# State-space tiles of a two-block layer: decay blocks in three buffers, the subtract of the next tile while on this one

## What is computed

```python
def step(state, inp):                       # one chunk of M_CHUNK = 128 tokens; 8 of them
    xc, ac, bc, cc = inp
    acum = jnp.cumsum(ac, axis=1)
    seg = jnp.where(causal, acum[:, :, None] - acum[:, None, :], -jnp.inf)
    scores = jnp.einsum('btgn,bsgn->btsg', cc, bc)[..., None] * jnp.exp(seg)
    y_diag = jnp.einsum('btsgh,bsghp->btghp', scores, xc)
    y_off = jnp.einsum('btgn,bghpn->btghp', cc, state) * jnp.exp(acum)[..., None]
    w_end = jnp.exp(acum[:, -1:] - acum)
    new_state = (state * jnp.exp(acum[:, -1])[..., None, None]
                 + jnp.einsum('bsgn,bsghp->bghpn', bc, xc * w_end[..., None]))
    return new_state, y_diag + y_off
```

## Time and profile before

| what | value |
|---|---|
| device time, median of 3 runs | 3124.95 us (3123.76 to 3127.22) |
| device time of the profiled execution | 3125.96 us |
| its span | 3124.3 us |
| PE busy | 2945.9 us (94%) |
| DVE busy | 1750.8 us (56%) |
| ACT busy | 1009.9 us (32%) |
| POOL busy | 414.3 us (13%) |
| mean granted PE clock | 0.972 |

### The profile page before, as it was taken

The page is one execution under the profiler, slowest core; times in us unless marked ns, Lnnn a source line. Parts: engine busy times, 40 slices in busy tenths (PEclk is TensorE's granted clock), DMA queues, the critical chain, the costliest instruction groups (busy, mean ns, idle before and its releaser), DMA issues.

```text
span 3124.3 us, 39886 instructions
## 1 busy us (share of the span) xinstructions
PE 2945.9 (94%) x16263; PEld 2297.6 (74%) x16263; DVE 1750.8 (56%) x1912; ACT 1009.9 (32%) x1309; POOL 414.3 (13%) x461
## 2 busy tenths in 40 slices
PE   2998999999999999999898999999979998999989
PEld 2885656667788888888777887878767886666667
DVE  5566726662455455543585747567454227676773
ACT  2123435551211111111233424234333114444452
POOL 0002000001011111100101112021101001332340
PEclk7998999999999999999899999999979999999999
DMA  6355011011133333321124223242311221212021
GB/s 229 108 169 132 4 28 29 8 28 41 48 115 120 115 101 111 116 76 47 36 65 128 80 83 107 68 135 75 107 56 37 98 88 61 68 35 68 35 74 61
DMA packets 245528, 249.16 MB, mean 80 GB/s; under 512 B 14021, under 2 KB 208418, under 8 KB 245378
## 3 DMA queue, kind: packets, MB, share of 16 engines
q1 hardware_dynamic: 221664, 170.39, 18.0%
q0 software_dynamic: 17680, 58.89, 6.3%
q10 hardware_dynamic: 6034, 17.74, 1.5%
HBM read 218.17 MB, written 26.45 MB: 78 GB/s over the span
## 4 chain that ended last, share of the span: by engine, by line
PE 79%; DVE 11%; issue 4%; ACT 4%; DMA 1%; ACTq 0%; SPq 0%; DVEq 0%
PE PU L973 16%; PE PU L975 16%; PE PU L974 16%; PE PM L1614 2%; PE PU L1592 2%; PE PU L1284 2%; DVE small L2757 2%; PE PM L1602 2%; PE PM L1634 2%; PE PM L1636 2%; PE PM L1635 2%; PE PU L987 2%; PE PU L1216 1%; PE PU L988 1%; PE PU L989 1%
## 5 line engine op out<-in xcount | busy, mean ns | idle before, releaser
L973 PE MATMUL PU<-hH,w_hi_t 128*128 128x512 f32 (+1 forms) x1872 | 739.1, 395 | 2.4 <-DVE w_lo_t L2349 2.4
L975 PE MATMUL PU<-hH,w_lo_t 128*128 128x512 f32 (+1 forms) x1872 | 730.7, 390 | 0.0
L974 PE MATMUL PU<-hL,w_hi_t 128*128 128x512 f32 (+1 forms) x1872 | 729.9, 390 | 0.0
L2349 DVE TENSOR_TENSOR w_lo_t<-w_raw,w_hi_t 128x1024 fp32r<-128x1024 f32 x181 | 228.6, 1263 | 357.4 <-ACT w_hi_t L1746 345.3
L973 PEld LDWEIGHTS PU<-hH,w_hi_t 128*128 128x128 f32 (+1 forms) x1872 | 351.4, 188 | 77.0 <-DVE w_lo_t L2349 3.8
L975 PEld LDWEIGHTS PU<-hH,w_lo_t 128*128 128x128 f32 (+1 forms) x1872 | 350.8, 187 | 76.0
L974 PEld LDWEIGHTS PU<-hL,w_hi_t 128*128 128x128 f32 (+1 forms) x1872 | 351.4, 188 | 72.2
L1746 ACT ACTIVATE w_hi_t<-w_raw 128x1024 fp32r<-128x1024 f32 x167 | 174.5, 1045 | 458.0 <-PE PU L975 356.3
L2825 DVE SCALAR_TENSOR_TENSOR xT<-PU,mod,xT 128x1024 f32<-128x1024 f32 x120 | 154.0, 1283 | 202.5 <-PE PU L975 202.5
L3106 DVE TENSOR_TENSOR_SCAN s_keep<-s_keep,zero 128x128 f32<-128x128 f32 (+7 forms) x128 | 180.6, 1411 | 2.0 <-POOL s_keep L928 2.0
L928 POOL TENSOR_SCALAR_AFFINE_SELECT s_keep<-s_keep 128x128 f32<-128x128 f32 x128 | 114.5, 910 | 501.5 <-ACT s_keep L2237 500.9
(11 more groups left out here) (419 smaller groups left out, 5003.8 us busy)
## 6 DMA issues: line engine op xcount, KB each, us to landing
ada_w<-in_ada_w_dram POOLq DMA_DIRECT2D x64, 384.0 KB, 4.0
w_raw<-in_w_gu_dram SPq DMA_DIRECT2D x44, 512.0 KB, 3.8
w_raw<-in_m_in_w_dram SPq DMA_DIRECT2D x40, 512.0 KB, 3.9
ada_w<-in_w_ada_dram POOLq DMA_DIRECT2D x32, 512.0 KB, 4.6
seg<-decay_sums SPq DMA_DIRECT2D x32, 512.0 KB, 4.7
w_raw<-in_w_down_dram SPq DMA_DIRECT2D x22, 512.0 KB, 3.4
w_raw<-in_w_in_dram SPq DMA_DIRECT2D x17, 512.0 KB, 3.9
ada_w<-in_w_ada_dram SPq DMA_DIRECT2D x16, 512.0 KB, 18.8
```

The lines of the kernel that those rows point to most:

```text
L973: mm(PU[0:width, up, half, :], whi, aH[:, k, cols], start=k == 0, stop=False)
L974: mm(PU[0:width, up, half, :], whi, aL[:, k, cols], start=False, stop=False)
L975: last = mm(PU[0:width, up, half, :], wlo, aH[:, k, cols], start=False, stop=k == kt - 1)
L2349: V.tensor_tensor(w_lo_t[:, p, 0:w], w_raw[:, p, 0:w], w_hi_t[:, p, 0:w].bitcast(F32), ALU.subtract)\
```

## The change

The blocks `seg` get a third buffer, tile c uses buffer c % 3. On SP the DMA of tile j+1's block is issued in step j, behind the factors and the panel of step j, for j = 1 to 6 (tiles 0 and 1 as before). On VectorE the subtract of tile c+1 stands in step c, behind `output(c-2)` and the split and ahead of `masked(c)`; that of tile 0 stands ahead of the loop. The masking of the scores into `cbm` moves from `segments` into `masked`, directly ahead of the multiply. On ScalarE the high part of a panel and the copy of a z unit are each issued ahead of the next tile's Relu and Exp. PE's order is the same.

```diff
-        seg = at("seg", A + 11264, [P, 2, 8, P])
+        seg = [at(f"seg{n}", o, [P, 8, P]) for n, o in enumerate((A + 11264, A + 12288, A + 16384))]
@@ SP
             def tile_decays(i, j):
+                if j >= 2:
+                    sp.wait_ge(bc_landed[j % 2], 16 * (4 * i + j // 2))
+                if j >= 3:
+                    sp.wait_ge(ss_y, TT * i + j - 2)
...
-                sp.dma_start(seg[:, j % 2, :, :].rearrange("p h t -> p (h t)"), src).then_inc(bc_landed[j % 2], 16)
+                sp.dma_start(seg[j % 3][:, :, :].rearrange("p h t -> p (h t)"), src).then_inc(bc_landed[j % 2], 16)
@@
                 for j in range(TT):
-                    if j >= 2:
-                        sp.wait_ge(ss_y, TT * i + j - 1)
-                    tile_decays(i, j)
-                    if j >= 2:
+                    if j < 2:
+                        tile_decays(i, j)
+                    else:
                         sp.wait_ge(ss_g, TT * i + j - 1)
                     tile_factors(i, j)
...
+                    if 1 <= j < TT - 1:
+                        tile_decays(i, j + 1)
@@ ScalarE
+                if i == 0:
+                    activate(i, 5)
+                decays(i, 0)
                 for c in range(TT):
-                    if c == 0 and i == 0:
-                        activate(i, 5)
-                    decays(i, c)
                     if c % 2 == 0:
                         split()
                     else:
                         p = unit()
                         free(af(zf[:, c // 2, :], unit_ps(p), ACT.Silu if last else ACT.Copy))
+                    if c + 1 < TT:
+                        decays(i, c + 1)
@@ VectorE
             def segments(i, c):
...
                                 acum[:, c, 8 * i:8 * i + 8].unsqueeze(2).broadcast_to([P, 8, P]), ALU.subtract).then_inc(ss_seg, 1)
+
+            def masked(i, c):
                 ve.wait_ge(ss_cb, TT * i + c + 1)
                 if TT * i + c:
                     ve.wait_ge(ss_m, TT * i + c)
                 V.tensor_tensor(cbm[:, :], PM[:, 3, 0:P], tri[:, :], ALU.mult).then_inc(ss_cbr, 1)
-
-            def masked(i, c):
                 ve.wait_ge(ss_exp, TT * i + c + 1)
@@
+                segments(i, 0)
                 for c in range(TT):
                     if c >= 2:
                         state_update(i, c - 2)
                         output(i, c - 2)
-                    segments(i, c)
                     if c % 2 == 0:
                         split()
                         skip()
+                    if c + 1 < TT:
+                        segments(i, c + 1)
                     masked(i, c)
```

More of the change, by code:

```diff
@@ L1482, in ssd_out @@
                         last = mm(PM[hd * HD:(hd + 1) * HD, 0, f * P:(f + 1) * P], xdt[:, h * HD:(h + 1) * HD],
-                                  seg[:, c % 2, h, :], start=True, stop=True)
+                                  seg[c % 3][:, h, :], start=True, stop=True)
                 last.then_inc(ss_y, 1)
@@ L2143, in decays @@
                 act.wait_ge(ss_seg, TT * i + c + 1)
-                s2 = seg[:, c % 2, :, :].rearrange("p h t -> p (h t)")
+                s2 = seg[c % 3][:, :, :].rearrange("p h t -> p (h t)")
                 link(af(s2, s2, ACT.Relu, scale=-1.0))
@@ L2932, in segments @@
                 ve.wait_ge(bc_landed[b], 16 * (4 * i + c // 2 + 1))
-                V.tensor_tensor(seg[:, b, :, :], seg[:, b, :, :],
+                V.tensor_tensor(seg[c % 3][:, :, :], seg[c % 3][:, :, :],
                                 acum[:, c, 8 * i:8 * i + 8].unsqueeze(2).broadcast_to([P, 8, P]), ALU.subtract).then_inc(ss_seg, 1)
+            def masked(i, c):
                 ve.wait_ge(ss_cb, TT * i + c + 1)
@@ L2938, in segments @@
                 V.tensor_tensor(cbm[:, :], PM[:, 3, 0:P], tri[:, :], ALU.mult).then_inc(ss_cbr, 1)
-            def masked(i, c):
                 ve.wait_ge(ss_exp, TT * i + c + 1)
                 ve.wait_ge(ss_cbr, TT * i + c + 1)
-                V.tensor_tensor(seg[:, c % 2, :, :], seg[:, c % 2, :, :], cbm[:, :].unsqueeze(1).broadcast_to([P, 8, P]),
+                V.tensor_tensor(seg[c % 3][:, :, :], seg[c % 3][:, :, :], cbm[:, :].unsqueeze(1).broadcast_to([P, 8, P]),
                                 ALU.mult).then_inc(ss_m, 1)
```

## The result

The changed kernel takes 3224.99 us (median of 4 runs, 3221.67 to 3226.57), the kernel before 3124.36 in the same comparison: a ratio of 1.0323, with a 95% interval of 1.0305 to 1.0341. It is 3.2% slower, some 101 us; 3228 was predicted. The span of its profiled execution is 3220.0 us, 95.7 more than that of before.

The account below looks back on a forecast made before the run. PE was taken as the bound. Scans before output(5) add 94 us and the ends 9, together 103 on the profiled 3126: 3229, less 1 for the median, 3228; range 3190 to 3268.

Parts of the forecast that it names:

- The bound: PE, busy 94% of the span, bounds the kernel; at 8.67 us a tile, some 27 us is the most won.
- The loop: Scans, c = 2 to 6: output(c-2), SP's issues, block landing, VectorE to output(c-1); 12.9 us a tile, 14.6 with a panel.
- the panel's term: Block behind factors and a panel on SP: issued at 2.51 us instead of 1.96, landing 6.1 us instead of 4.9.
- VectorE's part: VectorE behind the block's landing: subtract 1.13, mask 0.3, multiply to the end of output(c-1) 4.59 us.
- the upper end of the range: 3268 us: VectorE's instruction lengthened once a loop (+17), a panel's landing 6.8 (+6), half the way to (c).
- The skill's fit: Block's DMA by 2.0 us and 436 GB/s: 3.2 us for 512 KB instead of 4.9, the sum 34 us lower.
- PE in the loop: PE is in time with 5 us to spare and idles 4.2 us a tile at the scores, L1458.
- The first tile: Groups 1 to 3: PE stands still 6.8 us for cbm(0); output(0) ends 20.3 us behind the first subtract, not 13.8.
- The ends: Behind output(5): PE late for the last ssd_out, 3 us each in groups 0 to 2, hidden in group 3; 9 us.
- (c): Rival: waits drop TensorE's clock to 1.2 GHz, PE bounds the scans; 74 us more, 3300 at most; chance 0.11.
- (a): Rival: it gains, ScalarE's 2 to 3 us leaving VectorE's path, if blocks land within 2.65 us; 3099, chance 0.04.
- (b): Rival: the loop hides and only first tiles cost; 27 us won, 3 x (6.8 + 3) lost; 3128, chance 0.03.

Follow-up runs that it names:

- the last mended version: Changed kernel with blocks issued ahead of the factors' wait, scores masked ahead of the split, and each multiply ahead of the next tile's subtract: 3108.03 us, ratio 0.9951.
- late block: Changed kernel with the block of tile j+1, from tile 3 on, also waiting for ssd_out(j-1), as with two buffers: 3288.94 us, ratio 1.0521.
- the first experiment: Changed kernel with the block of tile j+1 issued, in steps 2 to 6, ahead of SP's wait for output(j-2) and the factors: 3134.25 us, ratio 1.0036.

## Why the prediction was right

**The bound.** PE was the bound, and at most some 27 us stood against the loss. Right: in the last mended version the five steps of the four groups fell from 199.2 to 172.9 us, 26.3 less. The total won 17, 15 of it in the scans, since the first tiles (60.0 for 56.0 us) and the last two outputs (58.6 for 51.3) took 11 us more; these two the bound left out.

**The loop.** 12.9 us a step without and 14.6 with a panel were predicted; the twelve steps without were 12.8 to 14.2, on average 13.4, the eight with 14.1 to 15.4, on average 14.4. Cutting the loop at SP's wait gave back 91 of 101 us, and shortening it by the factors 57. Its terms: the block's issue 2.0 us behind the output (1.96 predicted). The landing 4.0 to 6.1, on average 4.8 (4.9), behind a panel 5.3 to 6.3, on average 5.6 where 6.1 was taken from a single row; the panel's term was too large by 0.5. VectorE's part was the term too small: subtract to output end was 6.1 us where nothing disturbed it (6.02 predicted), but 6.6 in the step shown above, whose multiply took 1.68 in place of 1.22 us, and 6.6 on average of the twelve steps without a panel. In ten of these twelve the subtract or the multiply was lengthened, each time while GpSimd scaled inputs of a tile (here `xdt`, from 1700.03 on); in the eight with a panel, and in the other two, GpSimd did nothing then and neither was. Such collisions stood only at the upper end of the range, with 17 us; half of that should have been in the sum. The panel's error made up for a part only: five steps were 68.4 to 70.1 us for 67.9, 4.9 us more over the four groups.

**The skill's fit.** The runs have landings of 3.3 to 3.8 us where the DMA ahead had been issued 3.5 us or more earlier (all 20 late blocks) and 4.8 on average right behind them. By the fit of the Trainium skill (DMA: Bandwidth & Descriptors, Anatomy of one DMA), which is for DMAs that GpSimd issues, the landing is an estimated 3.2 us and the total by the prediction's sum 34 us lower, 3194. That sum took 1.7 us off all 20 landings; from 6.1 with a panel it would be 2.9, so 44 us. The fit is near for a lone block; what stands just ahead makes the rest. The rule of the Trainium skill (DMA: Bandwidth & Descriptors, Rules for kernel authors) to issue early and wait late was borne out by the size of the first experiment.

**PE in the loop.** Predicted were 4.2 us idle a tile, at the scores. The place is right (93.5 us in 25 waits), the size was 3.4: PE was idle for 17 us of five steps, because its own work took longer at the lower clock. That PE has time to spare held in the changed kernel: in none of the 20 steps did VectorE wait for PE, which is why the clock did not matter there. It no longer held once SP waited for PE: the late block.

**The first tile.** PE stopped for 7.0 us in group 1 (6.8 predicted) and came back at the lower clock: the half unit lost 7.79 - 5.81 = 2.0 us, where 3 had been taken from a longer stretch. VectorE's last piece took 0.7 us and not 1.3, since the copy was done while PE worked. So the end of `output(0)` was at 18.8 to 18.9 us, not 20.3. Group 0: 16.5 for 17.

**The ends.** 9 us predicted, 8.2 measured (51.3 to 59.5 in the table), but otherwise spread: 3 each in groups 0 to 2 and none in group 3 were predicted, 1.5, 3.0, 1.5 and 2.1 measured. That group 3 hides it was wrong.

**The sum.** 94 + 9 = 103 us in the scans were predicted, 102.6 measured. The median of the runs moved by 101. The mechanism was right, but so close a number is in part luck: the steps were 4.9 us more than predicted and the first tiles 4.7 less. Of the upper end of the range, 3251 of 3268 follow from terms with a size; "half the way to (c)" isn't worked out.

**The rivals.** (a), the gain, would have needed a block landed 2.65 us behind the output; it landed at 6 to 9. (b) fell with it: the loop wasn't hidden. (c), the clock: the granted clock in the five steps did fall to 0.88 to 0.90 (in groups 0 and 1 it was 1.00 before; windows of the changed kernel, from `output(0)` to `output(5)` of groups 0 and 1)

```profile
1666.00:1734.70 68.70, 51.92 (x275) 41.08 (x274) 34.59 (x45) 14.53 (x14) 11.24 (x10) 0.89 0.30 92
1881.40:1951.50 70.10, 52.89 (x272) 41.60 (x271) 34.05 (x44) 15.93 (x16) 10.86 (x11) 0.88 0.30 90
```

but PE was idle for 17 of 69 us all the same, so the low clock only ate into waiting. The Trainium skill (TensorE: Matmul & The Clock Gate, HAM oscillation) tells of a kernel whose clock falls again at every tile because of DMA waits; the trace agrees that it falls, though the half units lost between nothing and 2.6 us, and the loop here hides it. It did count in the late block's loop, where the half units of the 20 steps took 7.1 to 8.7 us in place of 5.81, 2.3 more on average.

**ScalarE.** I costed its part at nothing because a wait covered it. It is nothing for a simpler reason: the timelines of ScalarE over a scan list the same instructions in the same order before and after (Relu and Exp of tile 0, high part, Relu and Exp of tile 1, copy of z, and so on). The loop is only written from another point of the same sequence.

## What to carry to other kernels

A further buffer lets a load start earlier only if nothing else that stands ahead of it on the issuing queue waits for something later: read what the DMA's position hangs on, not what its own semaphore hangs on. When a consumer is moved ahead by one tile, its producer must move by as much, else a slack becomes a loop, and the loop's length (wait, issues, landing, the consumer's work to the next release) is the new time of a step. The longest wait of the bounding engine names where it stands still; whether what it waits for is the cause shows only when that is taken away alone.

## What the runs showed of the hardware

A block of 512 KB landed in 3.3 to 3.8 us when the DMA ahead of it had been issued 3.5 us or more before (the 20 late blocks), in 4.0 to 6.1 right behind 512 KB of factors (4.8 on average), and in 5.3 to 6.3 with a panel in between (5.6): what stands just ahead costs 1 to 2 us. Whether that is the order in the queue or the shared bandwidth, no run here separates. A 128x1024 subtract or multiply of VectorE took 1.3 to 1.9 us in place of 1.22 in the ten steps in which GpSimd scaled inputs at the same time. TensorE came back from waits of 6.9 to 7.1 us in groups 1 to 3 at a granted clock of 0.50, 1.2 GHz, and the next half unit took 7.8 to 7.9 us in place of 5.81; in the first experiment, behind waits of 6.8 to 6.9, it was 8.5 to 8.6. Kernels with the same instructions up to the first scan reached it up to 9.5 us apart, which is more than the whole effect of the smaller edits; their verdicts rest on the intervals and on the steps in the traces.
